# S5 impulse responses and input tables moved to other stages, a low-rank product on four column groups, head norms summed by VectorE

## The reference, cut to what matters

```python
mem_n = rms_norm(mem, mem_norm_w)
h = rms_norm(x, norm_w[0])
q, k, v, r, z, xq = split_cols(h @ w_in, [512, 512, 2048, 16, 3072, 1024])
g = log_sigmoid(r @ w_gate_up + gate_bias) / 16         # low-rank gate, rank 16
o = rms_norm(gla_chunked(q, k, v, g), out_norm_w)       # 4 heads of 512 values: the head norms
y = concat([o, memory_attention(xq, mem_n, w_kv)]) * silu(z)
x = x + y @ w_out
```

## Time and profile before

| what | value |
|---|---|
| median of 3 runs | 3040.07 us (3040.02 to 3040.38) |
| the profiled execution, its own time | 3043.74 us |
| its span, first to last instruction | 3041.9 us |
| TensorE busy | 2806.8 us, 92% of the span |
| mean granted TensorE clock | 0.971 of full |
| VectorE, ScalarE, POOL busy | 1405.3, 986.2, 1116.4 us |

### The profile page before, as it was taken

One profiled execution on the slowest core, in us unless ns is written; L12 is line 12 of the kernel. 1 busy time (PEld: TensorE's weight loads), 2 busy tenths in 40 slices (PEclk: granted clock), 3 DMA queues, 4 the chain that ended last, 5 costly groups with the idle time before them and its releaser, 6 DMA issues.

```text
span 3041.9 us, 49670 instructions
## 1 busy us (share of the span) xinstructions
PE 2806.8 (92%) x20286; PEld 2288.4 (75%) x20286; DVE 1405.3 (46%) x2208; ACT 986.2 (32%) x1526; POOL 1116.4 (37%) x821
## 2 busy tenths in 40 slices
PE   6988989989999999999989888899998998899997
PEld 4666567767777578787778877899997877678885
DVE  5788365510316611402138575660724356382452
ACT  3222354312212245423235333312124455332211
POOL 0233022366334189443433413344442321244442
PEclk9999999999999999999999998999999999899999
DMA  4889211245573379332322100222222210223322
GB/s 138 258 263 271 77 44 43 74 145 170 164 230 90 99 194 268 100 97 84 92 88 63 37 3 30 70 90 90 90 90 71 83 47 17 62 83 97 94 93 76
DMA packets 132306, 325.19 MB, mean 107 GB/s; under 512 B 54912, under 2 KB 56576, under 8 KB 131344
## 3 DMA queue, kind: packets, MB, share of 16 engines
q1 hardware_dynamic: 96128, 221.90, 24.6%
q0 software_dynamic: 31632, 88.21, 9.9%
q10 hardware_dynamic: 4352, 12.26, 1.1%
HBM read 288.32 MB, written 33.95 MB: 106 GB/s over the span
## 4 chain that ended last, share of the span: by engine, by line
PE 64%; DVE 17%; POOL 5%; ACT 5%; DMA 4%; issue 3%; DVEq 1%; ACTq 0%; SPq 0%; POOLq 0%
PE ps L270 16%; PE ps L273 16%; PE ps L275 16%; POOL ring_r L363 3%; DMA d_pb<-arena 3%; ACT high L372 1%; DVE h L603 1%; PE ps L925 1%; POOL d_k L1495 1%; PE ps L583 1%; PE ps L1790 1%; PE ps L2205 1%; PE ps L297 1%; PE ps L301 1%; PE ps L300 1%
## 5 line engine op out<-in xcount | busy, mean ns | idle before, releaser
L363 POOL TENSOR_TENSOR ring_r<-ring,high 128x1024 fp32r<-128x1024 f32 x335 | 828.0, 2472 | 1346.9 <-ACT high L372 1345.7
L270 PE MATMUL ps<-h_hi,high 128*128 128x512 f32 (+1 forms) x2104 | 736.8, 359 | 39.1 <-POOL ring_r L363 16.5
L275 PE MATMUL ps<-h_hi,ring_r 128*128 128x512 f32 (+1 forms) x2104 | 662.1, 349 | 0.0
L372 ACT ACTIVATE high<-ring 128x1024 fp32r<-128x1024 f32 x367 | 387.7, 1057 | 836.6 <-PE ps L270 699.4
L273 PE MATMUL ps<-h_r,high 128*128 128x512 f32 (+1 forms) x1912 | 643.7, 346 | 0.0
L270 PEld LDWEIGHTS ps<-h_hi,high 128*128 128x128 f32 x2104 | 399.7, 190 | 120.3 <-issue 44.5
L275 PEld LDWEIGHTS ps<-h_hi,ring_r 128*128 128x128 f32 x2104 | 369.9, 190 | 54.0
L273 PEld LDWEIGHTS ps<-h_r,high 128*128 128x128 f32 x1912 | 365.0, 191 | 41.7 <-issue 1.4
L273 PE MATMUL ps<-f_r,high 128*128 128x264 f32 (+1 forms) x960 | 294.9, 321 | 0.0
L270 PE MATMUL ps<-f_hi,high 128*128 128x264 f32 (+1 forms) x896 | 270.7, 316 | 2.2 <-POOL ring_r L363 1.8
L275 PE MATMUL ps<-f_hi,ring_r 128*128 128x264 f32 (+1 forms) x896 | 230.9, 316 | 0.0
(11 more groups left out here) (484 smaller groups left out, 4152.4 us busy)
## 6 DMA issues: line engine op xcount, KB each, us to landing
ring<-in_units SPq DMA_DIRECT2D x402, 512.0 KB, 3.6
d_ca<-arena POOLq DMA_DIRECT2D x16, 640.0 KB, 9.2
arena<-d_ca POOLq DMA_DIRECT2D x16, 640.0 KB, 5.1
arena<-d_q POOLq DMA_DIRECT2D x32, 256.0 KB, 8.2
d_pb<-arena POOLq DMA_DIRECT2D x16, 512.0 KB, 11.4
arena<-d_pb POOLq DMA_DIRECT2D x16, 512.0 KB, 4.2
arena<-d_ca POOLq DMA_DIRECT2D x16, 512.0 KB, 5.2
arena<-d_k POOLq DMA_DIRECT2D x128, 64.0 KB, 4.5
```

Source lines behind the costliest of these rows:

```text
L270: part = mm(acc, hi[:, cols], self.x_hi(k)[:, t0:t0 + tn], start=(k == 0), stop=False)
L275: ins = mm(acc, w[:, cols], self.x_hi(k)[:, t0:t0 + tn], start=False, stop=(k == self.kt - 1))
L363: eng.tensor_tensor(b.ring_r[:, slot, :], b.ring[:, slot, :], self.high[:, (j + self.flip) % 2, :], ALU.subtract).then_inc(b.unit_lo, 1)
L372: b.nc.scalar.activation(self.high[:, (j + self.flip) % 2, :], b.ring[:, u % RING, :], ACT.Copy).then_inc(b.unit_hi, 1)
```

## The change

It has six parts.

1. **Start.** The memory input goes first on SyncE's queue, and the loads that the first norm and the coefficients need go first on ACT's. The coefficients now come ahead of the memory norm on ACT and DVE. `mem_k` follows the memory norm at once, and the first norm's eight matmuls by ones lie between its eight outputs (`FirstNorm`). Its low parts are made by POOL. The keys and values keep a place of their own, so that the store and reload go away.
2. **Tables stage.** A block is now only `ca`. Its responses are computed at once: `Gemm.aside` calls `respond` on PE after every second unit, `keep_response` on ACT one block later, and POOL stores them (four transfers a block). `d_ca` holds 128 instead of 160 columns and is stored in pieces of 512 bytes. The stage's last response is kept and stored before ACT may keep the low-rank product.
3. **Input tables** (`S5InputTables`). `pb` of blocks 0 to 4 is made in halves during the tables stage (blocks 0 to 9 of `ca`), and `pb` of blocks 5 to 15 during `out0`, on DVE, with POOL's loads and stores.
4. **Low-rank product.** The same 16 matmuls, with weights padded to 32 columns, on four column groups; the gate matmul adds the four parts by contracting over 128 rows.
5. **Head norms** (`HeadNorm`). ACT makes four squares without a matmul between, DVE adds them (three 128x512 additions), and one matmul by ones follows a half tile of z. ACT's root moves to the next step.
6. **Split.** ACT makes the high parts of the gated tiles, five between two tiles of z; DVE only the low parts. `S5Responses` is gone from `out0`.

```diff
-        for k in range(KD):
+        for i in range(KD // QUARTERS):
             for part, h in enumerate((b.h_hi, b.h_r)):
-                ins = b.nc.tensor.matmul(b.ps[0:RANK, 0, :], m.w_rank[:, k, :], h[:, k, 0:L1].bitcast(F32),
-                                         start=(k + part == 0), stop=(k + part == KD))
+                for j in range(QUARTERS):
+                    k = i * QUARTERS + j
+                    ins = b.nc.tensor.matmul(b.ps[BAND * j:BAND * (j + 1), 0, :], m.w_rank[:, k, :],
+                                             h[:, k, 0:L1].bitcast(F32), start=(i + part == 0),
+                                             stop=(i + part == KD // QUARTERS))
...
+class HeadNorm(Rms):
...
+    def squares(self, act):
+        b, at = self.b, self.at
+        for s, v in self.needs:
+            act.wait_ge(s, v)
+        if at["summed"]:
+            act.wait_ge(b.summed, at["summed"])
+        for k in range(self.n):
+            if k == 3:
+                act.wait_ge(b.added, at["added"] + 1)
+            b.nc.scalar.activation(self.spot(k), self.x(k), ACT.Square).then_inc(b.squared, 1)
+
+    def add(self, dve, k):
+        b, at = self.b, self.at
+        dve.wait_ge(b.squared, at["squared"] + k + 1)
+        if k > 1:
+            dve.wait_ge(b.added, at["added"] + k - 1)
+        b.nc.vector.tensor_tensor(self.spot(0), self.spot(0), self.spot(k), ALU.add).then_inc(b.added, 1)
+
+    def tensor(self, pe):
+        b, at = self.b, self.at
+        for s, v in self.stay:
+            pe.wait_ge(s, v)
+        pe.wait_ge(b.added, at["added"] + self.n - 1)
+        b.nc.tensor.matmul(b.ps[:, self.banks[0], :], b.ones[:, :], self.spot(0), start=True, stop=True
+                           ).then_inc(b.summed, 1)
+
+    def roots(self, act):
+        b, at = self.b, self.at
+        act.wait_ge(b.summed, at["summed"] + 1)
+        if at["inverted"]:
+            act.wait_ge(b.inverted, at["inverted"])
+        b.nc.scalar.activation(b.root[:, 0:L1], b.ps[:, self.banks[0], :], ACT.Sqrt, bias=b.eps[self.eps],
+                               scale=1.0 / self.width).then_inc(b.rooted, 1)
...
-            if n >= 5 and n % 4 == 1:
-                self.rms[(n - 5) // 4].tensor(pe)
-            for s, half in halves[:-1]:
+            for i, (s, half) in enumerate(halves[:-1]):
                 z.half_tensor(pe, s, half)
+                if n >= 5 and n % 4 == 1 and i == 0:
+                    self.rms[(n - 5) // 4].tensor(pe)
...
+            self.split.high_group(act, s - self.PLAN[-1][-1] - 1)
...
+            pool.dma_start(b.d_ca[n], m.ca[par][:, :, 16:144]).then_inc(self.block_out[par], 16)
+            if n >= 2:
+                store_responses(n - 2)
+            if self.inputs.early(n - 1):
+                self.inputs.turn(pool, (n - 1) // 2)
+
+        def store_responses(n):
+            pool.wait_ge(self.k_kept, n + 1)
+            for j in range(QUARTERS):
+                pool.dma_start(b.d_k[n][:, j:8:QUARTERS], m.kpad[n % 2][32 * j + S5_H:32 * j + 32]
+                               ).then_inc(self.k_stored[n % 2], 16)
...
+    def respond(self, pe, n):
+
+        b, m, par = self.b, self.m, n % 2
+        pe.wait_ge(self.made, n + 1)
+        if n >= 2:
+            pe.wait_ge(self.k_kept, n - 1)
+        for g in range(8):
+            i, j = divmod(g, QUARTERS)
+            ins = b.nc.tensor.matmul(b.ps[32 * j:32 * j + 32, 4 + 2 * par, i * P:(i + 1) * P],
+                                     m.ca[par][:, g, P:P + 32], m.ca[par][:, g, 0:P], start=True, stop=True)
+        ins.then_inc(self.responded, 1)
...
+    def unit_tensor(self, pe, u):
+
+        n, second = divmod(u - self.beside[0].unit0, 2)
+        if second:
+            self.respond(pe, n)
+
+    def unit_scalar(self, act, u):
+
+        n, second = divmod(u - self.beside[0].unit0, 2)
+        if second and n >= 1:
+            self.keep_response(act, n - 1)
...
-            q, k = m.qk[par], m.bk[par]
-            t512 = m.tmp[:, 0:512]
-            pbv = m.pb[par].rearrange("p g (c q) -> p c g q", c=2)
-            eight = lambda ap: ap.rearrange("p (g q) -> p g q", g=8)
-            inner(tt(pbv[:, 0], eight(q[:, 0]), eight(k[0]), ALU.mult))
-            inner(tt(t512, q[:, 1], k[1], ALU.mult))
-            tt(pbv[:, 0], pbv[:, 0], eight(t512), ALU.subtract)
-            inner(tt(pbv[:, 1], eight(q[:, 0]), eight(k[1]), ALU.mult))
-            inner(tt(t512, q[:, 1], k[0], ALU.mult))
-            tt(pbv[:, 1], pbv[:, 1], eight(t512), ALU.add).then_inc(self.made, 1)
+                link(tt((bb, small)[c], f, bc, ALU.mult))
+            tt(bb, bb, small, ALU.add).then_inc(self.made, 1)
...
+    LATE = [1, 1, 2, 1, 2, 1, 2, 1]
...
+    def turn(self, pool, n):
+
+        pool.wait_ge(self.made, n + 1)
+        pool.dma_start(self.b.d_pb[n], self.buffers(n)[2]).then_inc(self.stored[n % 2], 16)
+        following = n + 1 if n < self.EARLY else n + 2
+        if following < (self.EARLY if n < self.EARLY else NB):
+            self.load(pool, following)
...
+            self.keys.out_tensor(pe, k)
+            pe.wait_ge(b.squared, rms.at["squared"] + k + 1)
+            b.nc.tensor.matmul(b.ps[:, rms.banks[0], :], b.ones[:, :], b.sq[:, k % 2, 0:L1],
+                               start=(k == 0), stop=(k == KD - 1)).then_inc(b.summed, 1)
...
+    def high(self, act, tiles):
+
+        for k in tiles:
+            act.wait_ge(self.gated.multiplied, k + 1)
+            self.b.nc.scalar.activation(self.hi(k), self.z(k), ACT.Copy).then_inc(self.b.out_hi, 1)
...
+        link(tt(to, eight(q[:, 0]), eight(k[:, c]), ALU.mult))
+        link(tt(tmp, q[:, 1], k[:, 1 - c], ALU.mult))
+        last = tt(to, to, eight(tmp), ALU.add if c else ALU.subtract)
```

474 lines of the change are left out of this document (284 added, 190 removed).

## The result

The changed kernel took 3014.4 us (median of four runs, 3009.3 to 3020.4) where the kernel before took 3040.05 in the same session: a ratio of 0.992, with a 95% interval of 0.989 to 0.994. In a second session five more runs gave 3008.7 us and 0.9905 (0.989 to 0.992). It is faster by about 0.9%, some 26 to 31 us. The forecast was 2976.5 us, with a range of 2957 to 3006. Less than half of the gain came, and the time lies outside the range.

The account below looks back on a forecast made before the run. The prediction took TensorE, busy 92% of the span, as the bound. Its terms summed to -63.5 us from 3043.74, giving 2980.2; less 3.7 for the median, the forecast was 2976.5 us, range 2957 to 3006.

Parts of the forecast that it names:

- Part 1: Start: ACT no longer waits for the last small load, so `mem_k` starts at 28.0 instead of 36.4 us; -5 us.
- Part 2: Tables stage: PE's gaps and half clock go, responses and some remaining wait come in; -17 us, between -25 and -7.
- I leave 1 to 1.5 us of wait in five blocks, 6 us in all: Tables stage: allowance for input-table loads landing later than DVE needs them, with 4 us more for half clock.
- the prediction's first sign of being wrong: Tables stage: the forecast is wrong if waits for a DMA landing stand on DVE.
- Rival A: Tables stage: the queue still holds DVE by late stores and loads; -4 instead of -17, time 2990 us; chance 0.09.
- Part 4: Low-rank product: column groups bring the first exponential 7.8 us after the end of `v`; -8 us, 0 to -10.
- Rival D: Low-rank product: the four column groups run in turn, giving -1 and 2983 us; chance 0.03.
- Rival C: Tables stage: storing `ca` in 512-byte pieces lands too late, PE waits some 5 us a block; about 3055 us; chance 0.03.
- Part 5: Head norms: one matmul by ones a head instead of four, less a wait for DVE's additions; -9 us, -4 to -12.
- Rival B: Output product: DVE and POOL hold each other up at each of eleven `pb` tables; 3004 to 3021 us; chance 0.11.
- Part 6: Start of output product: PE's wait for the second unit's low part shrinks to 2 us; -11.4 us, -6 to -13.5.
- Part 3's second half: Output product: responses, 8.6 us, and waits after eight outputs, 4.2 us, go, with DVE's table work covered; -13 us.

Follow-up runs that it names:

- e10_tables_spread: Changed kernel with four early input tables beside every third block instead of five beside every second, the fifth moved to `out0`; 2993.9 us.
- e5_no_table_loads: Changed kernel without the input loads of 13 of 16 tables and DVE's waits for them, arithmetic and stores kept, tables wrong; 2985.0 us.
- e12_lows_on_vector: Changed kernel with four early tables spread, norm matmul behind mixed matmuls, and DVE making z's last three low parts and `out0`'s first instead of POOL; 2981.2 us.
- e6_norm_after_mix: Changed kernel with DVE waiting for POOL's low parts ahead of z's, and each head's matmul by ones behind its mixed matmuls; 2996.5 us.

## Why the prediction was right or wrong

**Part 1 (-5, measured -4.0; -6.8 in the second session's profile, -7.2 in the best kernel, whose start is the same): right.** `mem_k` starts at 25.07 us, 3 us earlier than forecast, and a wait of 2.22 us for ACT's copies at 78.76 took some of that back.

**Part 2 (-17, measured -3.5): mis-sized, in one term.** The step that failed is "I leave 1 to 1.5 us of wait in five blocks, 6 us in all". It was 4.75 us in four blocks. The text had the load due 12 us after DVE finished a half and delivered after 13 to 15. It was due after 14.7 and delivered after 19.3, because POOL issues it only 5.7 us later, with eight other issues of its turn ahead, and it then needs 11.4. The sum took an average rate over a whole stage, and the loads come in a burst. "A wait of up to some 2 us does not reach PE" was right, a wait of 4.6 does, with half clock behind it. In the stage, PE was idle for 13.6 us and lost 8.5 to the clock (0.04 x 212.1), 12.1 more than the 10 that the sum left for both. The bound, -25 if no wait is left, is what `e10_tables_spread` and `e5_no_table_loads` gave; the sum's own terms without a wait are -27.2, so part of that agreement is luck. DVE waiting for a DMA landing in this stage was the prediction's first sign of being wrong, and it stood in the trace.

**Rival A** had the right size (-4) and the mechanism: the queue did hold DVE, by loads asked for late; of the stores that it named too, DVE waited for none. The change of order moved the wait to ACT.

**Part 4 (-8, measured -8.2): right**, with its reason. ACT's wait for the last block's store stands ahead of the copy (3.77 us), as the sum said, and ends earlier than forecast:

```profile
313.74 0.47 ACT L945 ACTIVATE p<-ps,negmax 128x256 f32<-128x256 f32 x1
```

The first exponential starts 6.3 us after the product, not 7.8, so by the prediction's own measure the part gave 9.6; a clock of 0.96 in the rest of the stretch took some back (with 1.00, in `e12_lows_on_vector`, it gave 9.5). The ratio of 3.1 for the responses is a slip: 0.109 / 0.034 is 3.2. Rival D did not happen. **Rival C** did not either: `d_ca` in 512-byte pieces landed in 4.9 us, where 18 would have decided.

**Part 5 (-9, measured +6.0): two steps failed.** The wait was forecast at 2.5 us and is 2.41, but the gain counted against it, "1.3 to 1.8 us at the first three heads, 3 at the last", came out at -0.3, 1.4, -2.1 and 2.7 us, 1.8 in all. It took the wait of the second head in the earlier trace rows for that of every head, where the third had none to lose, and it left the clock out: behind the gap at 426.90 the mixed matmuls take 0.64 us, where they take 0.46 elsewhere, and the same at the third head. Most of the -9 was there, but for a matmul behind the mixed ones (`e6_norm_after_mix`: 230.2 against 237.6 before, -7.4). The other 8 us, 5.79 of gap and 2.5 of half clock, are no part of the norms at all, but the low part of 8.37 us.

**Rival B** names that mechanism, DVE and POOL holding each other up, and it put it into `out0`, at each table. There POOL's low parts stay at 2.4 to 2.9 us, and DVE pays, with 2.69 for an operation of 0.69. Part 6 moved the highs of z to ACT, so that DVE's row of lows now runs beside z's last low parts; in the earlier trace rows the 7.00 us stood beside DVE's split of the same tiles, some 40 us later. The prediction took it as gone with the split's end and did not ask what the row would stand beside now.

**Part 6 (-11.4, measured -7.1): mis-sized, in the clock.** The gap is 2.86 us for a forecast of 2, which is 0.9 of the 4.3. The other 3.3 is the step "4.8 us are lost now", less the 1.5 kept. The window of 15.7 us has a clock of 0.79, but its 24 matmuls took 5.57 us, full speed; the low clock lay in the idle time, where (1 - c) x T counts it a second time. Behind the gap of 10.12 us before, eight matmuls ran at half clock, behind that of 2.86 us seven, so there was next to nothing to win.

**Part 3's second half (-13, measured -2.9): mis-sized, by one cover.** "DVE has at most 8.6 us of `pb` and 1.4 of its own in the 17 us of an output; that covers it" counts the arithmetic, which `e5_no_table_loads` bears out (-13.9 with all of it in place). It leaves out that the arithmetic waits for 1 MB of loads first, up to 9.60 us, and that POOL's next low part waits for the arithmetic. That made the three gaps, 7.1 us, and some 2.5 us of half clock. The sum had the terms for work and none for the wait.

**The sum.** Parts 2, 3 and 5 missed by 13.5, 10.1 and 15.0 us, part 6 by 4.3, part 1 by 1.0; the stretch that the change leaves alone gave 3.8. With the placements repaired and one table moved to `out0`, no part undone, the kernel takes 2981.2 us, 4.7 above the forecast. That is in part luck: the rest of `out0` still misses by 10, and the stretch left alone gives 8.5 in that profile. The range was too narrow because its lower parts were bounded one by one, while A's and B's mechanisms both came in at part of their price.

## What to carry to other kernels

A transfer that is hidden by arithmetic needs a line of its own in the sum: when it is issued (behind what, on which queue), when it lands, and when it is first wanted. Work taken off the bounding engine is worth its length only where its replacement is ready when that engine gets there; look for the place in the order where the engine waits anyway, and put it behind that. Read the wait at every place that the change touches, not at one of them. If a wait is removed by putting its transfer first in the queue, look at once at who owns what is now second. When a half-clock stretch is priced from a window's mean clock, take out the part of the window in which the engine was idle.
